# A 256-token two-block transformer kernel: part of each step's probability transpositions moved from before the scores to after them

## What is computed

```python
# first block: for each of 8 heads, c = 0, 1, causal, with a bias by distance
s = einsum('bhcqd,bhckd->bhcqk', q, k) * sm_scale + bias
p = softmax(s)
a = p[:, :, 0] - lam * p[:, :, 1]
out = einsum('bhqk,bhkv->bhqv', a, v)
# second block: 8 heads over blocks of 256 keys (all of them here), and
# 8 heads over the 64 keys that an indexer's scores choose for each query
logits = where(ok, einsum('bqhd,bqkhd->bqhk', q, k) * scale + bias, NEG)
out = einsum('bqhk,bqkhd->bqhd', softmax(logits), v)
```

## Time and profile before

| | |
|---|---|
| median of 3 runs | 951.77 us |
| the profiled execution's own time | 952.06 us |
| its span | 950.3 us |
| TensorE matmuls (PE) busy | 939.1 us, 99% |
| weight loads (PEld) busy | 831.3 us, 87% |
| vector engine (DVE) busy | 669.2 us, 70% |
| ScalarE (ACT) busy | 468.5 us, 49% |
| GpSimd (POOL) busy | 35.6 us, 4% |
| matmuls, line 845 (transpositions of the probabilities) | 72, 11.0 us busy |

### The profile page before, as it was taken

One profiled execution on the slowest core, in us unless ns is written; L12 is line 12 of the kernel. 1 busy time (PEld: TensorE's weight loads), 2 busy tenths in 40 slices (PEclk: granted clock), 3 DMA queues, 4 the chain that ended last, 5 costly groups with the idle time before them and its releaser, 6 DMA issues.

```text
span 950.3 us, 15363 instructions
## 1 busy us (share of the span) xinstructions
PE 939.1 (99%) x5891; PEld 831.3 (87%) x5891; DVE 669.2 (70%) x964; ACT 468.5 (49%) x722; POOL 35.6 (4%) x64
## 2 busy tenths in 40 slices
PE   9999999999999999999999999999999999999997
PEld 7988888888898988888887889899999888888886
DVE  5876767676787876667678587977876676666663
ACT  4544344445666444444445566566664454434432
POOL 2010002000000001000001000000000000000000
PEclk9999999999999999999999999999999999999999
DMA  8686666539533377655653945445565546655631
GB/s 295 204 287 224 198 222 210 198 135 264 154 130 105 114 249 249 223 195 180 217 178 103 264 134 133 144 137 165 178 216 184 191 140 214 204 183 189 206 135 44
DMA packets 141648, 175.67 MB, mean 185 GB/s; under 512 B 7152, under 2 KB 119985, under 8 KB 141598
## 3 DMA queue, kind: packets, MB, share of 16 engines
q1 hardware_dynamic: 138384, 166.55, 54.9%
q0 software_dynamic: 2656, 8.31, 2.5%
q10 hardware_dynamic: 558, 0.12, 0.1%
HBM read 173.88 MB, written 1.09 MB: 184 GB/s over the span
## 4 chain that ended last, share of the span: by engine, by line
PE 93%; DVE 5%; issue 1%; ACT 1%; POOL 0%; DVEq 0%; POOLq 0%
PE bank L507 91%; DVE w_lo L1148 1%; PE bank L845 1%; PE bank L639 1%; DVE x_rows L1570 1%; DVE x_rows L1577 1%; DVE stats L1562 1%; ACT w_hi L1136 0%; DVE x_both L1549 0%; DVE arena L2008 0%; PE bank L651 0%; ACT arena L1309 0%; DVE arena L1821 0%; PE bank L718 0%; DVE vareps L1538 0%
## 5 line engine op out<-in xcount | busy, mean ns | idle before, releaser
L1148 DVE TENSOR_TENSOR w_lo<-raw,w_hi 128x1024 fp32r<-128x1024 f32 x308 | 362.7, 1221 | 88.0 <-ACT w_hi L1136 87.5
L507 PE MATMUL bank<-x_both,w_hi 128*128 128x256 f32 (+2 forms) x2032 | 408.3, 325 | 0.0
L507 PEld LDWEIGHTS bank<-x_both,w_hi 128*128 128x128 f32 (+1 forms) x2032 | 336.6, 188 | 37.1 <-issue 5.5
L1136 ACT ACTIVATE w_hi<-raw 128x1024 fp32r<-128x1024 f32 x308 | 307.9, 1050 | 100.0 <-PE bank L507 95.7
L507 PE MATMUL bank<-x_both,w_lo 128*128 128x256 f32 (+1 forms) x1432 | 272.4, 281 | 0.0
L507 PEld LDWEIGHTS bank<-x_both,w_lo 128*128 128x128 f32 (+1 forms) x1432 | 217.0, 190 | 2.6
L507 PE MATMUL bank<-w_hi,arena_r 128*128 128x512 f32 x672 | 189.5, 390 | 0.2 <-DVE arena_r L1709 0.2
L507 PEld LDWEIGHTS bank<-w_hi,arena_r 128*128 128x128 f32 x672 | 124.6, 188 | 25.6 <-issue 0.8
L507 PE MATMUL bank<-w_lo,arena_r 128*128 128x512 f32 x336 | 106.2, 389 | 0.0
L1625 DVE TENSOR_REDUCE arena<-bank 128x512 f32<-128x1024 f32 x52 | 63.6, 1222 | 48.1 <-PE bank L507 48.1
L507 PE MATMUL bank<-w_hi,x_both 128*128 128x512 f32 (+1 forms) x352 | 75.8, 346 | 0.6 <-ACT w_hi L1136 0.4
(11 more groups left out here) (180 smaller groups left out, 599.4 us busy)
## 6 DMA issues: line engine op xcount, KB each, us to landing
raw<-w_up SPq DMA_DIRECT2D x76, 512.0 KB, 4.5
raw<-w_down SPq DMA_DIRECT2D x76, 512.0 KB, 4.3
raw<-w_in SPq DMA_DIRECT2D x60, 512.0 KB, 4.6
raw<-w_gate SPq DMA_DIRECT2D x44, 512.0 KB, 4.7
raw<-w_qkv SPq DMA_DIRECT2D x24, 512.0 KB, 4.7
raw<-w_o SPq DMA_DIRECT2D x16, 512.0 KB, 4.2
table<-bias_vectors POOLq DMA_DIRECT2D x12, 256.0 KB, 4.7
raw<-w_pa SPq DMA_DIRECT2D x4, 512.0 KB, 4.4
```

Source lines behind the costliest of these rows:

```text
L507: return nc.tensor.matmul(*a, skip_group_check=True, **k)
L1136: nc.scalar.activation(w_hi[slot][:, c], raw[slot][:, c], ACT.Copy).then_inc(hi_done, 1)
L1148: last = nc.vector.tensor_tensor(w_lo[slot][:, c], raw[slot][:, c], w_hi[slot][:, c].bitcast(F32), ALU.subtract)
```

## The change

In the twelve turns that have a unit, a step to apply and a step to score, TensorE makes two of the three blocks' transpositions ahead of the scores and the third behind them, directly before the unit's stream. In the second block a third is one block for each of the two heads, so four transpositions stay and two move. The wait for `prob_ready` stays with the first part, `turned` is signalled by the second part, and the wait for the copy of the step before (`pt_copied`, `pt_copied2`) stands in both. The other turns keep their order, and no other engine's code is changed.

```diff
--- before.py
+++ after.py
@@ -832,18 +832,20 @@
             if before and unit not in BANK5:
                 eng.wait_ge(proj_copied, before)
 
-        def pe_turn_probs(eng, a):
-
-            eng.wait_ge(prob_ready, a + 1)
+        def pe_turn_probs(eng, a, blocks=range(3)):
+
+            if 0 in blocks:
+                eng.wait_ge(prob_ready, a + 1)
             if 1 <= a <= A_MOBA:
                 eng.wait_ge(pt_copied, a)
             elif a > A_MOBA:
                 eng.wait_ge(pt_copied2, a - A_MOBA)
             for m in range(1 if a < A_MOBA else 2):
-                for b in range(3):
+                for b in blocks:
                     c = slice(b * P, (b + 1) * P)
                     last = nc.tensor.transpose(bank[6 + m][:, c], prob[:, m, c], ident[:, :])
-            last.then_inc(turned, 1)
+            if 2 in blocks:
+                last.then_inc(turned, 1)
 
         def pe_score(eng, a, unit):
             eng.wait_ge(proj_copied, COPIED[unit] + 1)
@@ -927,10 +929,13 @@
         def pe_mixer(eng):
             score_unit = {step_of(u): u for u in range(U_QI, U_GATE)}
             for unit, apply, score_step in TURNS[2:]:
+                split = apply is not None and score_step is not None
                 if apply is not None:
-                    pe_turn_probs(eng, apply)
+                    pe_turn_probs(eng, apply, range(2) if split else range(3))
                 if score_step is not None:
                     pe_score(eng, score_step, score_unit[score_step])
+                if split:
+                    pe_turn_probs(eng, apply, range(2, 3))
                 eng.wait_ge(lo_done, unit + 1)
                 s = unit % SLOTS
                 if unit in COPIED:
@@ -1069,8 +1074,9 @@
                 last.then_inc(psum_open, 1)
 
             for unit, apply, score_step in HEAD_TURNS[:-1]:
+                split = apply is not None and score_step is not None and unit is not None
                 if apply is not None:
-                    pe_turn_probs(eng, apply)
+                    pe_turn_probs(eng, apply, range(2) if split else range(3))
                 if unit is None:
                     eng.wait_ge(x_ready, 4 * O_NORM + 1)
                     open_tile(0)
```

## The result

The changed kernel takes 955.55 us (median of 7 runs, 955.20 to 955.66) against 952.28 for the kernel before in the same set: a ratio of 1.0031, 95% interval 1.0021 to 1.0041. It is 3.3 us slower. The forecast was 952.3, with a range up to 953.8.

A forecast was written before the change was run, and what follows sets the result against it. TensorE, busy 99% of the span, was taken as the bound. Terms of -0.55 + 0.22 + 0.52 + 0.33 = +0.5 us on the median of 951.77 gave 952.3 us, range 950.4 to 953.8.

The forecast's parts named there:

- Steps 1 and 2: Split turns: scores start 0.11 us earlier (mixer 0.22); moved transpositions cost that again behind them, but open loads save 0.055 each.
- the third rival: Split turns: the lead transposition's load is as long as a product's, so the 0.055 gains are missing; 953.0 us, chance 0.07.
- the 0.6 us for the waits' issue: Second half's wait on `pt_copied`: up to 0.05 us a turn if its issue isn't hidden; costed at 0, kept for the range.
- Step 3: Units 39 and 91: scores wait for ScalarE's copy and can't start earlier, so these turns lose 0.055 and 0.165 us.
- Step 4: Later `turned` delays the vector engine: TensorE loses 0.52 us after unit 42 and 0.33 after unit 44; mixer slack suffices.
- nowhere else anew: TensorE waits for line 1771 before unit 43's and the unitless turn's transpositions, 0.3 to 0.6 us each, with no other new waits.
- a sign of being wrong: In the profile after: more than three new waits would show the forecast wrong.
- Step 5: Split units' streams run at 113.5 or 117.5 ns a product; no average change taken, all short -1.25 us, all long +0.9.
- my first rival: A transposition at the head puts all or nearly all the streams in the short pitch; 951.0 us, chance 0.15.
- The rival on the slower side: The head stage's loop through the vector engine becomes the bound in every turn; +3 us, 954.8, chance 0.08.
- the five terms: Losses at five reads in the head stage under the slower rival: about 0.5, 0.3, 1.1, 0.2 and 0.9 us.

The follow-up runs named there:

- a1: The changed kernel plus one transposition of the identity directly ahead of the gate stage's 864 products: 952.01 us, 0.9999 of the kernel before.
- d2: The changed kernel plus two small identity matmuls ahead of the eight fp32 matmuls that precede the gate stage's stream: 956.09 us, 1.0031 of the kernel before.
- a4: The changed kernel with the first block's copy of the turned probabilities moved from the vector engine to ScalarE, behind its softmax: 954.28 us, 1.0021 of the kernel before.
- b1: The kernel before plus one transposition of the identity directly ahead of the gate stage's stream: 952.08 us, 0.9993 of the kernel before.
- b3: The changed kernel plus one fp32 matmul of the identity, not a transposition, ahead of the gate stage: 951.99 us, 0.9991 of the kernel before.
- c1: The changed kernel with the first block's copy on ScalarE and a transposition of the identity ahead of the gate stage: 950.63 us, 0.9976 of the kernel before.
- d1: The kernel before plus one transposition of the identity ahead of unit 100's stream only: 955.58 us, 1.0021 of the kernel before.
- d3: The kernel before plus two small identity matmuls ahead of the eight fp32 matmuls that precede the gate stage's stream: 955.83 us, 1.0017 of the kernel before.
- d4: The kernel before, nothing moved, with the first block's copy of the turned probabilities on ScalarE behind its softmax: 952.83 us, 1.0004 of the kernel before.
- b2: The kernel before, nothing moved, plus one transposition of the identity between scores and stream in the twelve turns: 955.53 us, 1.0021 of the kernel before.

## Why the prediction was wrong

**Steps 1 and 2 held.** The added open load of a transposition measured 0.055 us in every split turn where I looked (0.33 against 0.27; with two, 0.44 against 0.38), and two products behind it 0.48. From the first transposition to the second product a split turn that waits for nothing gained 0.04 to 0.05 us, so the size was right. A product in the same place pays 0.11 (in unit 40 of the kernel before, the first product behind the scores lasts 0.39 us and those in the stream 0.28), so the third rival, a lead load as long as a product's, fell. That the last score's matmul has drained before the next weights are loaded is shown by no run: behind the scores of a split turn that load starts 0.30 us after the last score's matmul starts, 0.07 ahead of the end that the trace gives it, in both kernels. No run shows the 0.6 us for the waits' issue in the range either: with the added wait in the changed kernel the same 0.30 us stand between the start of the last score's matmul and the next load as without it.

**Step 3 held.** In unit 91 the scores of the changed kernel stood idle for ScalarE's copy and began no earlier against it (the copy ends at 565.59); from the first transposition to the second product the turn lost 0.17 us, against the 0.165 of step 3:

```profile
565.64 0.93 PE L507 MATMUL bank<-arena 64*128 64x128 f32 x8 [0.16 <-ACT arena L1317]
...
566.50 0.44 PE L846 MATMUL bank<-ident,arena 128*128 128x128 f32 x2
```

**Step 4 held where it looked, and looked at too few turns.** Both turns that I named wait for line 1779, and the mixer's slack sufficed. From the last product of the stream ahead to the first transposition TensorE took 1.22 us in both where it had taken 0.78: 0.89 us lost together, against my 0.52 + 0.33. But "nowhere else anew" was wrong: the short pitch brought TensorE earlier to transpositions for the output projection (line 651, units 42 and 44), where the vector engine's line 1975 now ends last, and 0.32 us were lost at each. With the wait in unit 39 that makes five new waits, more than the three that I had named as a sign of being wrong.

I had priced the waits at the old pitch and the pitch apart from the waits. The head stage came to +0.6, which is what my own terms for it give (-0.275 + 0.055 + 0.85 = +0.63). Four of its streams became shorter by 0.2 us each at the same time, and that changed nothing, because from unit 41 on the vector engine's loop sets the stage's length: a shorter stream in a loop that another engine closes gives its time back as a wait. Two traces with the same instructions up to there show it. In a1 unit 43 ran long, the loss ahead of unit 44 shrank by 0.20 us, and the stage took 115.22 us from unit 38 to the output projection, against 115.24 in the changed kernel; in d2, with unit 39 long, it took 115.25. a4 shows the reverse: with the loop open, the stage falls by 1.7 us.

**Step 5 is the one that failed, in its scope.** I had found the two pitches, and that a stream keeps the one it starts with, but then counted only the twelve streams that the change touches, 0.2 us each. I wrote that it takes "no change on average"; they all went short, a gain of about 1.5 us if nothing had waited, which was my first rival. Unit 100, which the change does not touch, went short too; with units 92, 97 and 99 that is the 0.8 us that the mixer gave back. What I left out is that a stream of 864 products behind them, the gate stage, takes one of the two pitches as well, and that this one is worth 3.8 us, more than the whole range was wide. The sum has to be taken over every stream that comes after the first altered one. The rows were there: the stage ran at 113.3 ns a product for 860 products in the trace of before, and one look at whether other streams of that kind sat at the other pitch gave 4.5 ns times their count as the bound above. With it the range would have ended near 956 (952.3 and 3.9).

**The chance.** The rival on the slower side (the vector engine's loop in all turns) was not what made it slow; the loop did close, at 0.32 to 0.45 us a turn in the turns where it did. (Its sum was also off: the five terms make 3.0, and 2.7 with the gains taken off, so 954.4 and not 954.8.) The slowdown came from a mechanism that stood among my rivals as a gain.

**What stays open.** Shown: the gate stage's pitch makes the slowdown; an instruction at its head sets it short (a1, b1, b3, c1, four of four); without one, it was the opposite of unit 100's in all ten traces, and one instruction ahead of unit 100 turned both (d1). Not shown by a trace: that the upper heap of the kernel before itself is the long pitch; what speaks for it is that the instruction at the head leaves no such heap, and that d3 and d4, traced in theirs, are long. Not shown: what in TensorE holds the two pitches apart, why the opposite and not the same is taken up, what chooses the side at unit 97 in the kernel before, and why the added transpositions left four of the head streams long in b2 while the moved ones in the changed kernel made all six short, or all but one.

## What to carry to other kernels

When a stream of equal matmuls fills a stage, read its pitch, start to start, and not its busy share; if any stream of the same form shows a second pitch, every change ahead of a long stream carries the count times the difference as a risk, however small the change (here 863 times 4.5 ns, 3.9 us). If runs fall into two heaps, look for such a stream: one cheap instruction at its head may pin it (it did in a1, b1, b3 and c1), and changes should be compared with it pinned. And where a signal is moved behind other work, price it with the streams at the length that they will have, because a shorter stream uses up the very slack that was to hide the late signal.

## What the runs showed of the hardware that I had not expected

A stream of matmuls with 256 columns, each with its own load of 128 x 128 weights, at a granted clock of 1.00, has two stable pitches in these traces, 113.3 and 117.8 ns, and keeps one of them for as long as it lasts: 864 matmuls in this kernel, across 18 units, while the other engines' work and the transfers change. It can differ between two executions with the same instructions up to there: unit 43 is short in the changed kernel and long in a1. The draw is made within the first few products: in the kernel before, the gate stage's first ones are, behind a first distance of 306 ns, 116, 118, 122 and 119 ns apart and then 113; in the changed one they are 117 and 118 behind the first and stay so.
